# Softmax probabilities divided in place on VectorE and turned with the identity, instead of turned with a diagonal of inverse sums

## What is computed

```
s = einsum('bthr,bsr->bhts', q_lat, ckv) + einsum('bthe,bse->bhts', q_rope, krope)   # 8 heads, 512 x 512
s = where(key_pos <= query_pos, s, -inf)
o = einsum('bhts,bsr->bthr', softmax(s), ckv)                  # "prompt attention"

q = qm.reshape(b, t, 4, 128) * 128 ** -0.5
s = einsum('bthd,bmhd->bhtm', q, k)                            # 4 heads, 512 x 256
cross = einsum('bhtm,bmhd->bthd', softmax(s), v)               # "memory attention"
```

## Time and profile before

| | |
|---|---|
| median of 3 runs | 1052.25 us (1052.16 to 1054.77) |
| profiled execution | 1053.92 us, span of its trace 1052.1 us |
| TensorE busy | 962.1 us, 91% of the span |
| VectorE, ScalarE, GpSimd busy | 541.9, 428.7, 99.7 us |
| prompt stage | about 645 to 752.5 us |
| memory stage | about 752.5 to 829.7 us |

### The profile page before, as it was taken

One profiled execution on the slowest core, in us unless ns is written; L12 is line 12 of the kernel. 1 busy time (PEld: TensorE's weight loads), 2 busy tenths in 40 slices (PEclk: granted clock), 3 DMA queues, 4 the chain that ended last, 5 costly groups with the idle time before them and its releaser, 6 DMA issues. The chain is left out here.

```text
span 1052.1 us, 15830 instructions
## 1 busy us (share of the span) xinstructions
PE 962.1 (91%) x5821; PEld 857.7 (82%) x5821; DVE 541.9 (52%) x984; ACT 428.7 (41%) x700; POOL 99.7 (9%) x104
## 2 busy tenths in 40 slices
PE   6879899999899999999999897999658699999996
PEld 4669899999789899998999745888547588888884
DVE  4444535322265687878875354655456442223434
ACT  4655211122213666766764222544355432232310
POOL 0000202212000000000000010121455000000000
PEclk9989999999899999999999999999879799999998
DMA  6875232233443778877874161100243464314222
GB/s 233 359 266 193 81 113 81 80 99 103 193 154 97 228 241 247 245 241 248 248 244 131 54 243 40 46 16 1 100 132 129 155 182 144 120 41 143 78 81 100
DMA packets 74893, 155.99 MB, mean 148 GB/s; under 512 B 9064, under 2 KB 43305, under 8 KB 72696
## 3 DMA queue, kind: packets, MB, share of 16 engines
q1 hardware_dynamic: 74160, 150.25, 43.1%
q10 hardware_dynamic: 656, 4.72, 1.3%
HBM read 143.56 MB, written 11.50 MB: 147 GB/s over the span
## 5 line engine op out<-in xcount | busy, mean ns | idle before, releaser
L274 ACT ACTIVATE w_hi<-w_raw 128x1024 fp32r<-128x1024 f32 (+1 forms) x78 | 81.5, 1048 | 255.3 <-PE z_acc L68 140.2
L281 DVE TENSOR_TENSOR w_lo<-w_raw,w_hi 128x1024 fp32r<-128x1024 f32 (+1 forms) x78 | 95.9, 1231 | 167.8 <-ACT w_hi L274 167.7
L66 PE MATMUL z<-x_hi,w_hi 128*128 128x288 f32 x512 | 154.6, 302 | 0.0
L67 PE MATMUL z<-x_lo,w_hi 128*128 128x288 f32 x512 | 151.7, 296 | 0.0
L68 PE MATMUL z<-x_hi,w_lo 128*128 128x288 f32 x512 | 151.7, 296 | 0.0
L66 PE MATMUL z_acc<-x_hi,w_hi 128*128 128x288 f32 x384 | 113.8, 296 | 2.8 <-DVE w_lo L281 2.8
L67 PE MATMUL z_acc<-x_lo,w_hi 128*128 128x288 f32 x384 | 113.3, 295 | 0.0
L68 PE MATMUL z_acc<-x_hi,w_lo 128*128 128x288 f32 x384 | 112.9, 294 | 0.0
L66 PEld LDWEIGHTS z<-x_hi,w_hi 128*128 128x128 f32 x512 | 97.0, 190 | 3.4 <-issue 1.1
L67 PEld LDWEIGHTS z<-x_lo,w_hi 128*128 128x128 f32 x512 | 97.1, 190 | 1.3 <-issue 0.2
L68 PEld LDWEIGHTS z<-x_hi,w_lo 128*128 128x128 f32 x512 | 97.0, 189 | 0.0
(11 more groups left out here) (399 smaller groups left out, 2044.7 us busy)
## 6 DMA issues: line engine op xcount, KB each, us to landing
w_raw<-in_w_feat SPq DMA_DIRECT2D x56, 512.0 KB, 4.0
k_raw<-in_cache SPq DMA_DIRECT2D x128, 192.0 KB, 3.0
v_raw<-in_cache SPq DMA_DIRECT2D x128, 128.0 KB, 2.6
o_raw<-in_w_out SPq DMA_DIRECT2D x32, 512.0 KB, 3.9
w_raw<-in_w_mem_kv SPq DMA_DIRECT2D x16, 512.0 KB, 5.4
x_t<-in_xT SPq DMA_DIRECT2D x4, 1152.0 KB, 7.4
gate_spill<-gate_tmp SPq DMA_DIRECT2D x16, 288.0 KB, 3.6
mix<-gate_spill SPq DMA_DIRECT2D x4, 1152.0 KB, 14.3
```

The costliest lines, as they stand in the source:

```text
L66: pe.matmul(out, a[0], b[0], start=start, stop=False)
L67: pe.matmul(out, a[0], b[1], start=False, stop=False)
L274: act.activation(s.whi[:, u % SPL, 0:w], s.wraw[:, u % RAW, 0:w], ACT.Copy).then_inc(s.w_hi, 1)
L281: dve.tensor_tensor(s.wlo[:, u % RAW, 0:w], s.wraw[:, u % RAW, 0:w], f32(s.whi[:, u % SPL, 0:w]), ALU.subtract).then_inc(s.w_lo, 1)
```

## The change

VectorE's `inverse` takes the reciprocal and then multiplies the exponentials by it in place (prompt: one instruction of 128, 256, 384 or 512 columns for each row block; memory: four of 256 columns for each head). TensorE turns the divided tiles with the identity (`pe.transpose`). GpSimd makes no diagonals; it keeps two memsets in the prompt stage, and memsets and the odd units' low parts in the memory stage. The tiles `inv_sum_diag` and `m_inv_sum_diag` are gone. The number of tiles that are turned stays.

```diff
--- before.py
+++ after.py
@@ -1372,7 +1372,6 @@
         pr = sb("probs", [P, 2, TRI[4]])
         pth, ptl = sb("pt_hi", [P, 4, SEQ], F32R), sb("pt_lo", [P, 4, SEQ], F32R)
         st = sb("p_stat", [P, 2, 4, 4])
-        dg = sb("inv_sum_diag", [P, 2, 4, P])
         ps = lambda n, sh: ctx.enter_context(nc.psum_tensor(n, sh, F32))
         p_qk, p_s, p_t, p_o = ps("pa_qk", [P, 2, 512]), ps("pa_s", [P, 2, 512]), ps("pa_t", [P, 2, 512]), ps("pa_o", [P, 512])
         w_in = s.wqk_in
@@ -1393,13 +1392,6 @@
             def _(pool):
                 pool.memset(f32(pth[:, 3, 256:384]), 0.0).then_inc(zeroed, 1)
                 pool.memset(f32(ptl[:, 3, 256:384]), 0.0).then_inc(zeroed, 1)
-                for h in range(NH):
-                    if h >= 2:
-                        pool.wait_ge(t_ps, 4 * (h - 1))
-                    for i in range(4):
-                        pool.wait_ge(inv, 4 * h + i + 1)
-                        pool.tensor_scalar(dg[:, h % 2, i, :], s.ident[:], st[:, h % 2, 3, i:i + 1], None, ALU.mult).then_inc(scaled, 1)
-                pool.wait_ge(scaled, 4 * NH)
 
             def exps(act, h, i):
                 v = pr[:, h % 2, TRI[i]:TRI[i + 1]]
@@ -1477,6 +1469,9 @@
                 def inverse(h, i):
                     dve.wait_ge(exped, 4 * h + i + 1)
                     dve.reciprocal(st[:, h % 2, 3, i:i + 1], st[:, h % 2, 2, i:i + 1]).then_inc(inv, 1)
+                    dve.wait_ge(inv, 4 * h + i + 1)
+                    e = pr[:, h % 2, TRI[i]:TRI[i + 1]]
+                    dve.tensor_scalar(e, e, st[:, h % 2, 3, i:i + 1], None, ALU.mult).then_inc(scaled, 1)
 
                 def turned(h, j):
                     dve.wait_ge(t_hi, 4 * h + j + 1)
@@ -1552,8 +1547,8 @@
                             pe.wait_ge(t_lo, 4 * h + j - 1)
                         for i in range(j, 4):
 
-                            last = pe.matmul(p_t[:, j % 2, P * i:P * i + P], pr[:, h % 2, TRI[i] + P * j:TRI[i] + P * j + P],
-                                             dg[:, h % 2, i, :], start=True, stop=True)
+                            last = pe.transpose(p_t[:, j % 2, P * i:P * i + P], pr[:, h % 2, TRI[i] + P * j:TRI[i] + P * j + P],
+                                                s.ident[:])
                         last.then_inc(t_ps, 1)
 
                 def values(h):
@@ -1607,7 +1602,6 @@
         st = sb("m_stat", [P, 2, 4, 4])
         qp = [sb("q_pad_hi", [P, 2, 16 * QROW], F32R), sb("q_pad_lo", [P, 2, 16 * QROW], F32R)]
         pp = [sb("p_pad_hi", [P, 2, 4 * MROW], F32R), sb("p_pad_lo", [P, 2, 4 * MROW], F32R)]
-        dg = sb("m_inv_sum_diag", [P, 2, 4, P])
         gp = sb("g_probs", [P, MT])
         gst = sb("g_stat", [P, 2, 4])
         od = sb("o_diag", [P, MW])
@@ -1679,14 +1673,6 @@
                     kind, h = part[0], int(part[1:])
                     if kind == "U" and h % 2:
                         unit_low(pool, h)
-                    if kind != "S":
-                        continue
-                    pool.wait_ge(inv, h + 1)
-                    if h >= 2:
-                        pool.wait_ge(t_ps, h - 1)
-                    for i in range(4):
-                        pool.tensor_scalar(dg[:, h % 2, i, :], s.ident[:], st[:, h % 2, 3, i:i + 1], None, ALU.mult).then_inc(scaled, 1)
-                pool.wait_ge(scaled, 4 * MH)
                 pool.wait_ge(u_lo[1], UN // 2)
 
             @block.scalar
@@ -1761,13 +1747,15 @@
                     kind, n = part[0], int(part[1:])
                     if kind == "S":
                         dve.wait_ge(s_ps, n + 1)
-                        if n >= 2:
-                            dve.wait_ge(scaled, 4 * (n - 1))
                         dve.tensor_reduce(st[:, n % 2, 0, :], p_s[:].rearrange("p a (i m) -> p (a i) m", m=MT), AX, ALU.max).then_inc(s_mx, 1)
                         dve.wait_ge(s_mx, n + 1)
                         dve.tensor_scalar(st[:, n % 2, 1, :], st[:, n % 2, 0, :], -MSCALE, None, ALU.mult).then_inc(nmax, 1)
                         dve.wait_ge(exped, 4 * n + 4)
                         dve.reciprocal(st[:, n % 2, 3, :], st[:, n % 2, 2, :]).then_inc(inv, 1)
+                        dve.wait_ge(inv, n + 1)
+                        for i in range(4):
+                            e = pr[:, n % 2, i, :]
+                            dve.tensor_scalar(e, e, st[:, n % 2, 3, i:i + 1], None, ALU.mult).then_inc(scaled, 1)
                     elif kind == "V":
                         dve.wait_ge(t_hi, n + 1)
                         dve.tensor_tensor(ptl[:], p_t[:], f32(pth[:]), ALU.subtract).then_inc(t_lo, 1)
@@ -1824,8 +1812,7 @@
                             pe.wait_ge(t_lo, n)
                         for i in range(4):
                             for m in range(2):
-                                last = pe.matmul(p_t[:, m, P * i:P * i + P], pr[:, n % 2, i, P * m:P * m + P],
-                                                 dg[:, n % 2, i, :], start=True, stop=True)
+                                last = pe.transpose(p_t[:, m, P * i:P * i + P], pr[:, n % 2, i, P * m:P * m + P], s.ident[:])
                         last.then_inc(t_ps, 1)
                     elif kind == "W":
                         pe.wait_ge(t_lo, n + 1)
```

## The result

The changed kernel takes 1058.08 us (median of 5 runs, 1057.70 to 1059.25), the kernel before in the same comparison 1053.02 (5 runs): ratio 1.0048, interval [1.0034, 1.0063]. It is slower by 5 us, outside the forecast range. Its trace has a span of 1056.3 us against 1052.1.

What follows compares the result with a forecast made beforehand. A chain across three engines, not TensorE's busy share, was taken to bound the prompt stage. Prompt +2.0 and memory -1.4 gave +0.6 us, put on the 1052.25 median as 1052.9 us; range 1049.6 to 1056.8, chance within 0.3% 0.68.

Steps and rivals of the forecast that it cites:

- the chain's +0.24 a head: Prompt heads 1 to 6: `pt_lo` 0.28 us earlier, first scaling pair 0.52 longer; period 12.44 to 12.68, +1.4 us in all.
- head 0: First prompt head: no turn to gain from, the scaling pair delays the maximum that `scores(1, 1)` waits for, +0.7 us.
- iteration 7: Prompt iteration without a projection: VectorE's whole queue carries the later `mix` and the reciprocals-to-maximum time grows, +0.9 us.
- the tail: Last prompt turn, head 7: starts 0.2 us earlier without GpSimd's diagonals and its ten shorter tiles are exposed, -1.0 us.
- The prompt stage's +2.0: Prompt stage total in us: heads 1 to 6 +1.4, first head +0.7, last iteration +0.9, last turn -1.0.
- the rival: Prompt heads: clock falls in the 2.0 us hole, values and scores at 1.2 GHz, +1 us per head, 1060; chance 0.08.
- the dear scaling: Rival: VectorE's scalings cost up to 0.28 us more per head and the second pair outgrows its cover, 1056.5; chance 0.11.
- GpSimd's release: Memory stage: without diagonals GpSimd splits odd units earlier, unit 3 by 1.6 us, bringing unit 6's transfer forward, -1.5 us.
- The other turns (V0, V1, V2): Memory stage turns before the last: saved passes lie in front of waits that end elsewhere, no gain.
- S3's +1.0: Memory stage, last S part: 1.3 us of scalings ahead of the `mix` products and `m_pt_lo`, +1.0 us.
- V3: Last memory turn, exposed: 8 passes instead of 16, -1.35 us, less 0.45 for the half-speed clock, -0.9 us.
- TensorE's saving: Rival: the shorter turns reach the end, prompt stage loses 8.8 us and the last memory turn 1.35, about 1042; chance 0.10.

Runs made afterwards that it cites:

- e1: Changed kernel with 8 unused 512-column products filling TensorE's hole before the third value product in heads 0 to 6: 1052.32 us, ratio 0.9993.
- e9: Changed kernel with 16 unused identity transposes filling the same hole in heads 0 to 6: 1051.26 us, ratio 0.9987.
- e10: Changed kernel with 8 unused two-pass products with the identity filling the same hole in heads 0 to 6: 1051.40 us, ratio 0.9982.
- e2: Changed kernel with the turns of both stages made as two-pass products with the identity instead of transposes: 1057.70 us, ratio 1.0036.
- e6: Changed kernel with ScalarE turning columns 2 and 3 before `exps(h, 3)` and VectorE's scalings moved later: 1041.19 us, ratio 0.9890.
- e7: Kernel before the change with only ScalarE's order moved, `exps(h, 3)` behind the turning of columns 2 and 3: 1046.97 us, ratio 0.9941.
- e12: Kernel of e5b with one identity transpose per tile in the prompt turn instead of a two-pass product: 1067.43 us, ratio 1.0137.
- e5b: Kernel of e2 with three unused VectorE instructions (0.81 us) ahead of the 512-wide maximum, widening the hole: 1063.70 us, ratio 1.0100.
- e11: Kernel of e5b with each two-pass product of the prompt turn replaced by two identity transposes: 1062.44 us, ratio 1.0089.
- e8: Changed kernel with GpSimd again making the memory stage's four diagonals of each S part, unused: 1064.16 us, ratio 1.0104.

## Why the prediction was wrong

- **Right: prices and passes.** One pass for each tile, scalings of 0.29, 0.35, 0.42 and 0.49 us, the chain's +0.24 a head (12.44 to 12.65, +0.21), the hole of 2.0 us with `pt_lo` as releaser.
- **Right: head 0 (+0.74 against +0.7)**, from the stage's start to the first turn: 668.10 - 645.06 and 667.42 - 645.12. **Right only in sum:** iteration 7 and the tail, +0.9 and -1.0, were +0.5 and -0.6 with the clock full (e1). The prompt stage's +2.0 without clock falls came in e9 (+2.0) and e10 (+2.2).
- **Wrong, and decisive: the clock.** The step that failed is that the sum has no term for the clock in the prompt stage: it let the stage keep 2.4 GHz with holes of 2.0 us, and I gave the rival 0.08, on the ground that the mean was 0.98 with holes of 0.66 us. That row could not speak for a hole three times as long, as the text itself noted. The place (values and scores behind the hole) and the price (about 1 us a head; 1.5 measured, in three heads, and 1.9 in the tail) of the rival were near. Together 6.4 us; without them the kernel is level with the one before (e1). The range ended at 1056.8, the dear scaling (1056.5 by its own sum), and left this rival's 1060 outside.
- **Wrong in size: the memory stage, -3.5 instead of -1.4.** GpSimd's release was -2.0 up to D0 (-1.4 to -2.2 over the kernels without diagonals), not -1.5 (unit 3 ended 1.75 us earlier within the stage, 1.6 forecast). The step that failed is "The other turns (V0, V1, V2) save passes in front of waits that end elsewhere: nothing", together with S3's +1.0: V2 to D1 became -1.0 instead. With transposes it is 1.53 us shorter than with two-pass turns (e2), 0.9 of it the turn itself; the rest goes with which of VectorE and GpSimd splits first, whose cause is open. V3 and what follows gave -0.6, not -0.9; the clock was 1.00 while V3 ran and fell right behind it.
- **The other rivals** did not come: the scaling was not dearer, the transpose was one pass, and TensorE's saving arrived at 0.3 of 1.1 us.

The two errors have opposite signs. The forecast with the clock's 6.4 us and the memory stage's -2.1 is 1052.9 + 4.3 = 1057.2, 1 us below the measured median.

## What to carry to other kernels

When a change takes work from the engine whose clock is throttled and leaves its chain as long as it was, ask where the idle time goes: gathered in one hole of some 2 us it cost 6.4 us, more than the 3.5 that the memory stage gained, and no hole of 1.2 us was followed by a fall. Before shortening the busiest engine's work, shorten the chain across the others, here by moving `exps(h, 3)` and the scalings behind what the next value product waits for; the change was then worth 5.8 us (e6 against e7). Where two engines shut each other out, taking work from the one that nobody waits for can be the better half of a change (the memory stage's 3.5 us, 2.0 of them up to D0).

## What the runs showed of the hardware

- A hole of 2.0 us was followed by a fall of the clock three times in six (changed kernel), one of 2.8 us met one also three times in six (e12), and 2.0 us with ten passes more in the head and a period of 13.74 none in six (e5b, e11); after a fall TensorE ran at 1.2 GHz for 3 to 3.5 us in the heads of the changed kernel, though busy all the time.
- Filling the hole with transposes or with products kept the clock equally: 1051.26 and 1051.40 us.
- An f32 tile turned by the identity as a transpose took one pass of 0.11 us; the same product as a matmul took two (e2: 20 passes, 1.72 us for the first 14).
- VectorE's scaling of four columns, 0.17 us alone, took 2.12 us beside GpSimd (e8); its 1024-wide subtraction, 1.22 alone, averaged 2.27 in a pair when GpSimd's came between (e2).
